# A four-layer streaming encoder step: maps of the differential and latent layers left unscaled, casts on ScalarE, the latent keys' rotation inside the scores

## What is computed

```python
def _rmsnorm(x, g):
    xf = x.astype(jnp.float32)
    return xf * lax.rsqrt(jnp.mean(xf * xf, axis=-1, keepdims=True) + EPS) * g
...
# B: differential attention, 6 heads with two maps each
p = jax.nn.softmax(s, axis=-1)
p_diff = p[:, 0] - lam * p[:, 1]
o = jnp.einsum('bhqk,bkhe->bqhe', p_diff, vv)
o = _rmsnorm(o, sub_g) * (1.0 - lam_init)
...
# C: latent attention, 12 heads; 64 plain and 32 rotated columns of q and k
s = (einsum(qn, k_nope) + einsum(rope(q_r), kr_all)) * scale
p = jax.nn.softmax(where(_chunk_mask(q_pos, k_pos), s, NEG), axis=-1)
o = jnp.einsum('bhqk,bkhd->bqhd', p, v)
```

## Time and profile before

| | us |
|---|---|
| median of 3 runs | 3321.17 (3317.43 to 3321.68) |
| profiled execution, its own time | 3319.59 |
| its span on the core | 3317.7 |
| TensorE busy | 2822.7 (85%) |
| weight loads busy (beside it) | 2631.0 (79%) |
| VectorE busy | 1540.5 (46%) |
| ScalarE busy | 1216.2 (37%) |
| GpSimd busy | 834.4 (25%) |
| mean clock granted to TensorE | 0.91 |

### The profile page before, as it was taken

How to read it: one execution, slowest core, us unless ns; L and a number is a source line. 1 busy time by engine, 2 the same in 40 slices (tenths; PEclk the granted TensorE clock), 3 DMA queues, 4 the chain that set the end, 5 groups by cost and what they waited for, 6 DMA issues and landing times.

```text
span 3317.7 us, 46359 instructions
## 1 busy us (share of the span) xinstructions
PE 2822.7 (85%) x18786; PEld 2631.0 (79%) x18786; DVE 1540.5 (46%) x3502; ACT 1216.2 (37%) x2680; POOL 834.4 (25%) x434
## 2 busy tenths in 40 slices
PE   4888999978979889879888677777779888999987
PEld 4788999978878878869877566667669788999877
DVE  7205565551135666751222256665651215655542
ACT  3323444432234444442232234434341224444431
POOL 7522222204322122204311222222203312212212
PEclk8999999989989999979997878888879999999989
DMA  3311111113111111113110000000013111111111
GB/s 143 101 49 38 54 51 45 55 63 103 40 39 49 55 58 52 49 62 94 54 39 27 23 13 9 6 9 6 14 49 98 55 39 51 45 47 59 51 66 65
DMA packets 55892, 167.90 MB, mean 51 GB/s; under 512 B 6464, under 2 KB 14272, under 8 KB 55168
## 3 DMA queue, kind: packets, MB, share of 16 engines
q1 hardware_dynamic: 55680, 164.94, 14.7%
HBM read 131.13 MB, written 33.79 MB: 50 GB/s over the span
## 4 chain that ended last, share of the span: by engine, by line
PE 64%; DVE 17%; ACT 10%; issue 4%; POOL 4%; DMA 1%; SPq 0%; DVEq 0%; ACTq 0%
PE acc L1363 30%; PE acc L1342 9%; PE acc L1426 8%; PE scores L1384 8%; PE turned L1396 5%; ACT prob L957 5%; DVE prob L1155 3%; DVE pt_split L1185 3%; PE scores L1295 2%; POOL h_split L1237 2%; DVE raw L1043 2%; ACT pt_split L966 2%; DVE prob L1178 2%; DVE prob L1175 1%; POOL w_lo L1229 1%
## 5 line engine op out<-in xcount | busy, mean ns | idle before, releaser
L1363 PE MATMUL acc<-h_split,w_hi 128*128 128x352 f32 (+3 forms) x5116 | 1263.3, 330 | 84.4 <-POOL w_lo L1229 40.6
L1363 PEld LDWEIGHTS acc<-h_split,w_hi 128*128 128x128 f32 x5116 | 899.6, 194 | 109.0 <-POOL w_lo L1229 44.4
L1229 POOL TENSOR_TENSOR w_lo<-w_raw,w_hi 128x1024 fp32r<-128x1024 f32 (+2 forms) x172 | 390.1, 2271 | 1946.5 <-ACT w_hi L916 1946.5
L1363 PE MATMUL acc<-h_split,w_lo 128*128 128x352 f32 (+3 forms) x2558 | 833.2, 326 | 0.0
L957 ACT ACTIVATE prob<-prob,stat 128x256 f32<-128x256 f32 (+9 forms) x576 | 386.0, 671 | 532.1 <-DVE stat L1155 532.0
L1426 PE MATMUL acc<-pt_split,v_split 128*64 128x256 f32 (+4 forms) x3486 | 487.4, 280 | 73.5 <-DVE pt_split L1185 63.5
L1185 DVE TENSOR_TENSOR pt_split<-turned,pt_split 128x512 fp32r<-128x512 f32 (+4 forms) x564 | 303.0, 552 | 519.3 <-ACT pt_split L966 518.7
L1363 PEld LDWEIGHTS acc<-h_split,w_lo 128*128 128x128 f32 x2558 | 496.2, 194 | 0.0
L1426 PEld LDWEIGHTS acc<-pt_split,v_split 128*64 128x64 f32 (+1 forms) x3486 | 389.2, 156 | 98.5 <-DVE pt_split L1185 81.0
L1396 PE MATMUL turned<-ident,prob 128*128 128x128 f32 (+2 forms) x1866 | 301.4, 287 | 147.4 <-DVE prob L1179 86.2
L1155 DVE CUSTOM_DVE_ANT_0 prob<-scores,bias 128x256 f32<-128x256 f32 (+9 forms) x576 | 338.1, 633 | 186.2 <-PE scores L1384 182.9
(11 more groups left out here) (102 smaller groups left out, 2805.4 us busy)
## 6 DMA issues: line engine op xcount, KB each, us to landing
w_raw<-w SPq DMA_DIRECT2D x148, 512.0 KB, 3.5
x_scr<-y_sb SPq DMA_DIRECT2D x24, 528.0 KB, 5.3
y_sb<-x_scr SPq DMA_DIRECT2D x24, 528.0 KB, 5.7
bias<-rel_in SPq DMA_DIRECT2D x24, 320.0 KB, 4.2
raw<-kcache SPq DMA_DIRECT2D x18, 256.0 KB, 3.8
v_cache<-vcache SPq DMA_DIRECT2D x18, 256.0 KB, 3.7
y_sb<-x_in SPq DMA_DIRECT2D x8, 528.0 KB, 5.9
y_out<-raw SPq DMA_DIRECT2D x8, 528.0 KB, 2.7
```

Source lines behind the costliest of these rows:

```text
L1229: pool.tensor_tensor(w_lo[:, n % 2, 0:wide], w_raw[:, n % 2, 0:wide], w_hi[:, n % 2, 0:wide].bitcast(F32), ALU.subtract).then_inc(wlo_made ...
L1363: ins = pe.matmul(acc[s.bank][:, 0:s.cols], (w_hi, w_lo)[ws][:, w, 128 * k:128 * k + 128], x(xs, k), start=k == 0 and y == 0, stop=k == s. ...
```

## The change

1. In C the maps aren't scaled. The high half of V gets 64 columns of ones beside each head's 64, so the product also gives each query's sum in rows 64 to 127 of `acc[0]`; ScalarE takes its logarithm and the exponential of minus that (1/sum), VectorE multiplies the gate with the unscaled result and then (new item emul) with 1/sum. The sum of the exponential's instruction is no longer asked for.
2. In B the first map stays unscaled; the second is multiplied by -lambda times the ratio of the sums. The result is larger by the first map's sum S, and its norm takes that out if epsilon becomes epsilon S squared: ScalarE squares S for each tile (scaled by the root of 128 epsilon), TensorE adds it to the sum of squares with one small matmul a tile.
3. N of the next unit's first tile moves from chunk 1 to chunk 0, of the second to chunk 1. Units run 1, 2, 0, 3, decoded; `BESIDE` changes; `prob` shrinks to 4928 columns.
4. conv's high halves move to ScalarE, part 0 is 512 tokens and keys (C: half of each).
5. In C the query rows are multiplied by the table as VectorE reads them from PSUM (now for uqe and uqo in place of ScalarE), and not added; the rotated keys stand twice (rows 64 to 95 and 96 to 127), so the contraction over 128 rows adds. Item rot goes.
6. The products with V run pass by pass over a chunk, the two with the map's high half first; only the third pass waits for the low half.

Left out below: buffer addresses, the layout of V's halves, new semaphores, and ScalarE's wait ahead of a weight's high half (for `side_ready` of the uqe or uqo chunk that last used the buffer).

```diff
+PV_PASSES = ((0, 0), (1, 0), (0, 1))
...
-PROB = 5632
+PROB = 4928
...
-    for g in (0, 1, 2, 3) if job.kind == "M" else (0, 2, 1, 3):
+    for g in (0, 1, 2, 3) if job.kind == "M" else (1, 2, 0, 3):
...
-BESIDE = {"M": (1, 1, 1, 0, 0), "A": (2, 2, 2, 2, 1), "B": (2, 2, 2, 2, 1), "C": (3, 4, 4, 3, 1)}
+BESIDE = {"M": (1, 1, 1, 0, 0), "A": (2, 1, 3, 2, 1), "B": (2, 1, 3, 2, 1), "C": (3, 3, 5, 3, 1)}
...
-            if s.what in ("uqe", "uqo"):
-                self.order.append(("rot", s.job, int(s.what == "uqo")))
+            self.last_side[s.weight] = s
             self.used(s.weight)
...
-        order.append(("evac", last))
+        order += [("evac", last), ("emul", last)]
...
                     self.scores(nxt, 0)
                 if narrow:
                     self.scores(nxt, 1)
+                if prev is not None:
+                    order.append(("emul", prev))
...
                     order += [("N", nxt, t) for t in range(2)]
+                if n > 1 and nxt is not None:
+                    order.append(("N", nxt, 0))
                 for x in parts[0][1:]:
                     self.part(*x)
...
             else:
-                if c == 1 and nxt is not None:
-                    order.append(("N", nxt, 0))
-                if c == (1 if n == 2 else 2) and two:
+                if c == 1 and two:
                     order.append(("N", nxt, 1))
...
-        return (slice(0, 256), slice(0, 256)) if part == 0 else (slice(256, TOK), slice(256, KEYS))
+        return (slice(0, 512), slice(0, 512)) if part == 0 else (slice(512, TOK), slice(512, KEYS))
...
-            half, quarters = TOK // 2, slice(0, 1) if part == 0 else slice(1, 4)
-            q, k = slice(part * half, part * half + half), slice(0, CHUNK_KEY) if part == 0 else slice(CHUNK_KEY, KEYS)
+            half, quarters = TOK // 2, slice(2 * part, 2 * part + 2)
+            q, k = slice(part * half, part * half + half), slice(2 * part * CHUNK_KEY, 2 * (part + 1) * CHUNK_KEY)
...
-            return [(qe_raw[0:96, q], q_sp[0:96, 0, q], q_sp[0:96, 1, q]),
+            return [(qe_raw[:, q], q_sp[:, 0, q], q_sp[:, 1, q]),
...
-                    (qo_raw[0:96, part, :], qo_sp[0:96, 0, q], qo_sp[0:96, 1, q]),
+                    (qo_raw[:, part, :], qo_sp[:, 0, q], qo_sp[:, 1, q]),
...
                 _, s, part, parts = item
-                if part == parts - 1:
+                if part == parts - 1 and s.what not in ("uqe", "uqo"):
                     read_side(s)
...
+                    if u.job.kind != "C":
+                        act.activation(p, p, ACT.Exp, scale=-1.0, bias=stat[0:tile.rows, i:i + 1],
+                                       accum_out=stat[0:tile.rows, 8 + i:9 + i]).then_inc(exps_ready.mark(tile.n, lane), 1)
+                    else:
+                        act.activation(p, p, ACT.Exp, scale=-1.0, bias=stat[0:tile.rows, i:i + 1]).then_inc(
+                            exps_ready.mark(tile.n, lane), 1)
...
+            elif name == "conv":
+                _, job, part = item
...
+                    elif job.kind == "C":
+                        act.wait_ge(*side_read.upto(job.sides["ck"][-1].n))
+                        act.wait_ge(*side_turned.upto(job.sides["uqo"][-1].n))
...
+                for i, (x, hi, _) in enumerate(splits_of(job, part)):
+                    act.activation(hi, x, ACT.Copy).then_inc(operand_hi.mark(job.n, part, i), 1)
...
-                act.activation(v_sp[0:rows, 0, block:block + n, :],
-                               t_ps[a % 2][0:rows, 0:128 * n].rearrange("p (n d) -> p n d", d=128),
+                act.activation(halves_of_v(job.kind, rows, block, n)[0], split_v(t_ps[a % 2][0:rows, 0:128 * n]),
                                ACT.Copy).then_inc(turned_hi.mark(a), 1)
...
+            elif name == "N" and item[1].job.kind == "B":
+                _, u, t = item
+                i, tile = stat_at(u, t), u.tiles[t]
+                act.wait_ge(*exps_ready.upto(tile.n, 1))
+                act.activation(sum_square(u, t), stat[0:tile.rows, 8 + i:9 + i], ACT.Square,
+                               scale=math.sqrt(128 * EPS)).then_inc(sums_squared.mark(tile.n), 1)
...
+            elif name == "evac" and item[1].job.kind == "C":
+                u = item[1]
+                act.wait_ge(*pv_done.upto(u.chunks[-1].p))
+                if u.before.job.kind == "C":
+                    act.wait_ge(*o_read.upto(u.before.n))
+                for lane in range(2):
+                    act.activation(recip[64 * lane:64 * lane + 64, 0:u.qn], acc[0][64:128, 256 * lane:256 * lane + u.qn],
+                                   ACT.Ln).then_inc(sums_logged.mark(u.n), 1)
+                act.wait_ge(*sums_logged.upto(u.n))
+                act.activation(recip[:, 0:u.qn], recip[:, 0:u.qn], ACT.Exp, scale=-1.0).then_inc(sum_recips.mark(u.n), 1)
...
-                act.activation(out, t_ps[u.sum_turn % 2][:, 0:u.qn], ACT.Ln, scale=1.0 / 128,
-                               bias=eps_sb).then_inc(b_logged.mark(u.n), 1)
+                act.activation(out, t_ps[u.sum_turn % 2][:, 0:u.qn], ACT.Ln, scale=1.0 / 128).then_inc(b_logged.mark(u.n), 1)
...
+                    for i, keys in enumerate((k_sp, ko_v)):
+                        for row in (64, 96):
+                            dve.tensor_copy(keys[row:row + 32, 0, :], raw[1][64:96, :]).then_inc(keys_roped.mark("hi", i), 1)
...
+                    for i, keys in enumerate((k_sp, ko_v)):
+                        dve.wait_ge(*keys_roped.upto("first lo", i))
+                        dve.tensor_copy(keys[96:128, 1, :], keys[64:96, 1, :].bitcast(F32)).then_inc(keys_roped.mark("lo"), 1)
...
+                _, s, part, parts = item
...
+                if s.what in ("uqe", "uqo") and part == parts - 1:
+                    half, cols = TOK // 2, slice(s.a, s.a + s.cols)
+                    if s.what == "uqe":
+                        dst = qe_raw[:, cols]
+                    else:
+                        dst = qo_raw[:, s.a // half, s.a % half:s.a % half + s.cols]
+                    if s.chunk == 0:
+                        dve.wait_ge(*operand_lo.upto(s.job.before.n, 1))
+                    dve.wait_ge(*side_ready.upto(s.n))
+                    dve.scalar_tensor_tensor(out=dst, in0=acc[s.bank][:, 0:s.cols], scalar=SCALE_C, in1=rope_sb[:, cols],
+                                             op0=ALU.mult, op1=ALU.mult).then_inc(side_turned.mark(s.n), 1)
...
-            elif name == "rot":
-                _, job, head = item
-                dve.wait_ge(*side_read.upto(job.sides["uqo" if head else "uqe"][-1].n))
...
-                _, job, part = item
...
-                for i, (x, hi, _) in enumerate(splits_of(job, part)):
-                    dve.tensor_copy(hi, x).then_inc(operand_hi.mark(job.n, part, i), 1)
...
+            elif name == "N" and item[1].job.kind != "C":
...
-                if u.job.kind == "B":
-                    lam_inverse = stat[0:rows, 24 + i // 2:25 + i // 2]
-                    dve.tensor_scalar(lam_inverse, inverse[1], neg_lam[0:rows, :], None, ALU.mult).then_inc(
-                        lam_recips.mark(tile.n, 0), 1)
-                    dve.tensor_scalar(p[0], p[0], inverse[0], None, ALU.mult).then_inc(lam_recips.mark(tile.n, 1), 1)
-                    dve.wait_ge(*lam_recips.upto(tile.n, 1))
-                    dve.scalar_tensor_tensor(out=p[0], in0=p[1], scalar=lam_inverse, in1=p[0],
-                                             op0=ALU.mult, op1=ALU.add).then_inc(probs_ready.mark(tile.n), 1)
-                else:
+                if u.job.kind != "B":
                     dve.tensor_scalar(p[0], p[0], inverse[0], None, ALU.mult)
                     dve.tensor_scalar(p[1], p[1], inverse[1], None, ALU.mult).then_inc(probs_ready.mark(tile.n), 1)
+                    continue
+                lam_ratio = stat[0:rows, 24 + i // 2:25 + i // 2]
+                dve.tensor_scalar(lam_ratio, inverse[1], neg_lam[0:rows, :], stat[0:rows, 8 + i:9 + i],
+                                  ALU.mult, ALU.mult).then_inc(lam_recips.mark(tile.n), 1)
+                dve.wait_ge(*lam_recips.upto(tile.n))
+                dve.scalar_tensor_tensor(out=p[0], in0=p[1], scalar=lam_ratio, in1=p[0],
+                                         op0=ALU.mult, op1=ALU.add).then_inc(probs_ready.mark(tile.n), 1)
...
-                dve.wait_ge(*pv_done.upto(u.chunks[-1].p))
...
                 else:
+                    if u.job.kind == "C":
+                        dve.wait_ge(*sums_logged.upto(u.n))
+                    else:
+                        dve.wait_ge(*pv_done.upto(u.chunks[-1].p))
                     for lane in range(2):
                         gate = y_sb[64 * lane:64 * lane + 64, u.job.tile, q]
                         ins = dve.tensor_tensor(gate, acc[0][0:64, 256 * lane:256 * lane + u.qn], gate, ALU.mult)
-                    ins.then_inc(o_read.mark(u.n), 1)
```

(50 more changed lines are left out.)

104 lines of the change are left out of this document (54 added, 50 removed).

## The result

The changed kernel takes 3208.2 us (median of four, 3206.0 to 3211.7) against 3320.1 for the kernel before (four, 3317.4 to 3321.7): ratio 0.9665, 95% interval 0.965 to 0.968. It is 112 us faster; 3150 us and a gain of 170 were forecast, in a range from 3065 to 3250. The profiled execution took 3211.7 us, its span 3209.4.

What follows compares the result with a forecast made beforehand. TensorE was held by waits on VectorE and the low clock behind them. Gains of 102 (C jobs), 26 (B jobs), 5 (C's start), 34 (last jobs), 22 (memory heads), minus 7 (A), sum 182, cut to 170: 3150 us, range 3065 to 3250.

Steps and rivals of the forecast that it cites:

- memory heads: Memory heads of each layer: a third of 28 us gained in C, 4 in each other layer, 22 in all.
- Step 1: Layer C, maps unscaled: 10.7 us a job leave VectorE; ones columns cost 1 us a job.
- Step 2: Layer C, rotation in the scores: 8.3 us a job of chains go, 128-row contraction costs zero, C's start gains 5.
- Step 3: Casts to ScalarE: VectorE loses 10 us a job in C, 2 in A/B; C stalls 1.5 us twice a job.
- Step 4: Layer B, first map unscaled: one of three scaling operations goes; TensorE's added small matmuls cost 3 us a job.
- Step 5: Unit order with sooner scaling: B's stall goes; costs 0.6 us a job in A, 0.9 in B, 1.5 in C.
- Step 6: Products with V by pass: 63.5 us of low-half waits can shrink by up to 0.7 us each; no separate term.
- Last jobs: Last job of each layer: 12 us gained in B, 12 in C, 5 in each A, 34 together.
- C stays bound by its score banks and ScalarE: Rival in layer C: shared score banks and ScalarE's load limit the gain to 8 us a job, 3218 us; chance 0.17.
- The new first unit stalls: Rival in A and B: each job stalls 3 us and pays 2.4 of clock, 3235 us; chance 0.09.
- The ScalarE queue that was to make it slower: Rival: cast blocks hold up turned maps in A and B and eat most of C's gain, 3364 us; chance 0.06.
- my two signs of error: Wrong if A's jobs lengthen by over 2 us, or C's new ScalarE waits exceed 8 us a job.

Runs made afterwards that it cites:

- e2: Changed kernel with C's maps scaled by VectorE, and the old order of units and old spread of projections in all layers: 3154.6 us.
- e1: Changed kernel with only C's maps scaled by VectorE again, without ones columns and logarithms: 3218.7 us.
- e3: Changed kernel, but in C ScalarE reads one more latent key chunk before the widest tile's exponentials: 3194.2 us.
- e5: e2 with the rotation undone: ScalarE reads the query chunks, VectorE rotates them, scores contract over 96 rows: 3217.1 us.
- e6: e2 with the high halves of queries and keys cast by VectorE again: 3163.9 us.
- e9: e2 with each block of four casts on ScalarE in C cut in two, a turned map's copy between: 3153.4 us.
- e8: e2 with the scaling product of layer B's first map put back: 3168.8 us.
- e7: e2 with the scaling of each tile's maps one chunk later, as in the old kernel: 3239.6 us.
- e4: Changed kernel with the scaling of each tile's maps one chunk later again: 3245.3 us.
- e12: e9 plus passes inside blocks in B, and one of the widest tile's two exponentials in C moved behind a copy: 3146.3 us.
- e11: Changed kernel with only the decoded unit of each latent job scaled by VectorE, its products taking 64 stationary columns: 3201.2 us.

## Why the prediction was right in sign and too large by 58 us

**The whole.** From e2, the undone parts cost: sooner scaling 85, rotation 62, passes 15, B's first map 14, casts 9, together 185; undone all at once with C's ones columns never there they are the 166 us between e2 and the kernel before. That this is near the forecast's gain (182, cut to 170) is in part luck: I had priced the parts otherwise, the largest of them not at all. The changed kernel adds the ones columns, 10 us faster (e1), and the new order of units, 64 us slower (e1 against e2). The step that failed is number 5: "that costs 0.6 us a job in A, 0.9 in B, in C 1.5". It measured 2.5, nothing and 4.2 (in C with VectorE scaling; with ones columns only the part of e3, 2.7, is shown).

By layer, the 182 were 11 in both A layers, 42 in B and 129 in C. The measured are minus 6.5, 42 and 74. In C, the jobs are 6.3 us longer than forecast (34 us), its start misses 8.5 and its memory heads 5.

**Step 1, C unscaled.** The 10.7 us a job that leave VectorE are there (7.3 net of its new work), but bring 10 us in all. I had let C fall to its full-clock work plus named stalls whichever part freed VectorE; after the rotation had gone, VectorE was idle 35 of 79 us a job and the scaling was on the path for 2.4. The ones columns were counted at 1 us a job, 0.01 on each matmul. TensorE's busy time rose 1.8, and in the decoded unit each such product was 50 ns dearer, not 10. The bound by the wide products was the wrong nearest row for products of 32 columns.

**Step 2, rotation.** 62 us, 11.8 a job, more than its 8.3 us of chains: it cuts a stall of 4.0 us to 1.3, ends one of 2.7, and with them the low clock behind both. Zero for the contraction over 128 rows holds (512-column score matmuls in C take 0.40 us each and start 0.23 us apart, as with 96 rows). C's start, "5 us gained", is the other sign: from the first product of the key rotation to the first low half of the queries it is 33.5 us, 30.0 before. VectorE's time line in the changed kernel:

```profile
1856.92 1.25 DVE L1083 TENSOR_TENSOR raw<-c_latents,rope_sb 32x1056 f32<-32x1056 f32 x1 [4.87 <-POOL h_split L1300]
...
1870.16 0.95 DVE L1169 SCALAR_TENSOR_TENSOR q_even_raw<-acc,rope_sb 128x352 f32<-128x352 f32 x2
```

and TensorE:

```profile
1870.73 0.95 PE L1429 MATMUL acc<-h_split,w_hi 128*128 128x352 f32 x2 [8.24 <-DVE q_even_raw L1169]
```

The first query chunk, for which TensorE waited 4.4 us before, is now read behind 13.2 us of work on the keys. It isn't the move of the read to VectorE that did this: the read waited for the keys when ScalarE did it too. So it was in the kernel before, with 9.2 us of work on the keys,

```profile
1906.09 0.82 ACT L876 ACTIVATE q_even_raw<-acc 128x352 f32<-128x352 f32 x2 [13.21 <-DVE h_split L1075]
```

and so it is in e5, where the keys are written twice and ScalarE reads:

```profile
1848.73 0.96 PE L1434 MATMUL acc<-h_split,w_hi 128*128 128x352 f32 x2 [8.38 <-ACT q_even_raw L911]
```

The keys' second copies are in the path, as I had it, with 4 us. The two chains that I set against them were not: they ran beside TensorE's projections, and from TensorE's restart to the first low half it was 20.1 us with them and is 19.7 without.

**Step 3, casts.** In C the move neither gains nor costs. The 1.5 us twice a job that I charged to turned high halves are not what the blocks cost: those waits are 10.5 us in four jobs with the casts on ScalarE (e2), on VectorE (e6) and with cut blocks (e9). The blocks hold up the read of a latent chunk, 1.2 us a job, and the cut gives 0.9 back. In all, the casts on ScalarE save 9 us. The Trainium skill (ScalarE: Activation LUTs, Rules for kernel authors) names `relu`, `max`, `min`, `add` and `mul` for VectorE, with a ratio for bf16, and no casts; I had stretched it to them. This case gives the stretched rule no support, since both engines idle 31 to 36 us a job in C (e2) and the kernel is 9 us slower with the casts on VectorE. My reading of the slow casts (2.41 and 1.34 us beside GpSimd) holds, with one correction: the cast of 1312 columns that took 0.84 us was not beside an idle GpSimd (GpSimd was at work for 0.67 of it), and the row of 2.41 us is VectorE's and says nothing of ScalarE's ports.

**Step 4, B's map.** Forecast for B in all 5 us a job; measured 6.5, and 2.0 of them are this step, by e8. B's jobs were right in sum (layer B minus 42, as 26 + 12 + 4 foretold), and it is luck that they were. The new order would have ended B's stall as I wrote, if the scaling had stayed late (69.9 to 66.5, e7 and e4); but the sooner scaling, which had no term, does it by itself (69.9 to 65.1), and behind it the order gives B nothing.

**Step 5, the second half.** Scaling one chunk sooner had no term of its own, it was named with the order, and is the largest part of the change: 37 us in the changed kernel, 85 in e2.

**Step 6.** 15 us in place of nothing of its own; in B it costs 4.

**Other terms.** Last jobs: B 13.7 us (from the key store to the end of the stream, 89.2 to 75.5), C 11.3, forecast 12 each; A 2.2 for 5. The memory heads, from ScalarE's table load on: in A and B 3.7 less to the first low half of the layer's own queries, forecast 4; in C 5 less to the last gate product of the second memory job (98.9 to 93.9), forecast 10.

**The rivals.** "C stays bound by its score banks and ScalarE" came nearest in mechanism, with the wrong resource: the bank of the projections and ScalarE's queue, not the score banks (1.2 us a job). C saved 12.6 a job, between its 8 and the forecast's 19. "The new first unit stalls" is real in A at half its price. The ScalarE queue that was to make it slower doesn't show: in the steady jobs of A TensorE waits for nothing on ScalarE, as "covered" said. Of my two signs of error one came: C's new waits on ScalarE sum to 8.9 us a job (18.9 + 6.8 + 5.2 + 4.7 over four), more than 8. The other, A's jobs longer by over 2 us, stayed below it with 1.6. Of what the forecast would show, the engines' busy times, C's clock (0.94) and the absence of waits on scaled maps there came; C's jobs (79.3 for 73), B's (64.9 for 66 to 67) and A's (longer by 1.6, not within 1) did not.

**Open.** The ones columns with the old order don't fit, so it isn't known whether they would gain there. Nor is it known what part of A's 2.5 us is the spread of projections and what the order itself: e2 undoes both, and the size of the map ring with them.

## What to carry to other kernels

When several edits free the same engine, don't add their work: list the waits in order and ask which edit ends which; the first to end them (here the sooner scaling and the rotation) takes the gain, and the rest is worth what it removes beyond that. Moving work to the smallest unit of a schedule moves it to where an in-order reader has least time, so look for what stands ahead of each read on its engine. Where a change bundles an order with a timing, run each alone: here the timing was worth 85 us in the old order and the order cost 64 with the timing early, but in B each would have done most of the other's work.

## What the runs showed of the hardware that I had not expected

- Thirty matmuls of 32 moving columns took 3.46 us at full clock where 20 of them had 128 stationary columns and 2.45 where all had 64, so 50 ns for each of the 20 (by their mean durations 271 and 212 to 217 ns).
- Fifteen such matmuls took 2.32 us ordered by passes and 1.92 block by block, both at full clock.
- TensorE ran 1814 matmuls of layer B in 251.1 us at granted clock 1.00 and in 257.4 at 0.98, with the same one stall of 0.8 us a job, by their order alone. The lower clock came in stretches of 3.4 us right behind the narrow products of the decoded unit, with TensorE busy all the while (3.40 of 3.40 us).
- A cast of 128x528 on VectorE took 0.42 or 1.54 us in the same kernel, beside GpSimd's subtractions; where it was short, a subtraction of GpSimd took 2.4 us in place of 1.3.
- The same stretch of instructions at C's head (second memory job to first latent job) took 185.1, 185.2 and 185.0 us in e3, e5 and e12 and 188.4 to 188.6 in the changed kernel, e1, e2 and e8 to e11. The difference lies ahead of the key rotation, where none of these edits reaches.
